# Dilated attention by token parity: four key blocks for every batch, probabilities divided before they are turned, values as the stationary operand

## The chip, the cores and the metric

One NeuronCore of a Trainium2 chip. The metric is the device time of the whole program in microseconds (us). The kernel before takes 1828.92 us, the median of 3 runs (1828.26 to 1829.07).

## The reference

A two-layer decoder trunk, 256 tokens, width 1024, float32. Each layer: RMSNorm, one input projection, multi-head latent attention (MLA, 8 heads) beside dilated window attention (3 groups of 8 heads), gates, output projection, then a dense feed-forward block (layer 0) or 8 experts (layer 1), then a gated embedding. The dilated part is what matters here:

```python
DIL_CONFIGS = ((128, 1), (512, 4), (2048, 16))     # window, dilation
# per group: tokens of one phase (token index modulo the dilation) attend to each other
dist = qi + span - kj
valid = (dist >= 0) & (dist <= span) & (blk * span - span + kj >= 0)
s = jnp.where(valid, q @ k * 64 ** -0.5 - slope * dilation * dist, -jnp.inf)
m = jnp.max(s); e = jnp.exp(s - m); den = jnp.sum(e)
o = (e / den) @ v;   lse = m + jnp.log(den)
# the three groups' outputs of head h are weighted by softmax over their lse
```

A weighting by the softmax of the three lse is the same as one softmax over the keys of all three groups together: one row of scores, one maximum, one sum. With dilation 4 or 16 a query sees only keys whose index has its own parity; with dilation 1 it sees the last 128 tokens of both parities.

## The kernel before

All big matrix products are made in three parts, high × high, high × low and low × high, from float32 halves. Weights come as a stream; ScalarE rounds each unit of 1024 words to its high half (`split_to`, L702), VectorE takes the rest as the low half (L1206), and `unit` on TensorE (L1874) runs 12 matmuls of 512 columns over it (L1885, L1886, L1911), for two token tiles. Rings of four units lie between them. No scheduler is at work: each engine's list is written out by hand in `attn`, once per layer, and semaphores bind the lists.

The change lies in the stretch of dilated attention. There `DIL_BATCHES` has 16 batches per layer, one for a query tile of 128 tokens and one head: tile 0 sees 128 keys in each of the three groups, tile 1 sees 256. Two batches (tile 0 of one head, tile 1 of its neighbour) share a pass of scores, one head in each half of the array's rows (`dil_term`, `scores_pair`, L2068). Then, per batch: `prep` on VectorE adds distances and masks and takes the maximum (L1365, L1369); `exps` on ScalarE (L820) makes the exponentials and their sum; `turn_probs` on TensorE transposes 3 or 6 blocks (L2093); `pt_evac` on ScalarE copies them (L831, L833); `values` on TensorE multiplies with the turned probabilities as the stationary tile and 64 columns of values moving (L2111); `normalise` on VectorE divides by the sum (L1382, L1383). When four batches are done, `o_dil_turn` transposes their two heads' outputs (L2149), and `od_round` and `od_rest` split them (L844, L1403). `round_pair` and `rest_pair` split the next two heads' queries and keys (L849, L1391).

Between these pieces TensorE runs "fill" units, the gate projections and then the branch projections (`FILL_AT`, `fill_unit`, `branch_unit`): one unit between two batches. `OM_AT`, `OD_AT` and `SPLIT_AT` say behind which batch the output turns and the splits stand. Before the stretch, V is projected by 12 units (`cols`, L1941) with contiguous blocks of 128 tokens as stationary tiles, and ScalarE scales it by the row's RMS factor while it copies it out (L777); the factors come from POOL (L515).

Of the kernel before, what the change touches and what calls it, by code (L numbers as in the profile page):

```python
# [22 lines left out]
P = 128  # L23
D = 1024
# [41 lines left out]
BRANCH_BANKS = ((2, 3), (0, 1), (7, 4), (2, 3))  # L66
# [31 lines left out]
def trunk_kernel(nc, x, p, positions, attn_norm, q_norm, kv_norm, ffn_norm, router_w, router_b, ple_norm,  # L98
                 final_norm, stream, out):
    ctx = ExitStack()  # L100
    with ctx:
# [33 lines left out]
        o_dil = sb("o_dil", [P, T, 512])  # L135
# [3 lines left out]
        dist = sb("dist", [P, DG, 256])  # L139
# [8 lines left out]
        rq8 = sb("rq", [P, 2, T])  # L148
        r2 = sb("r2", [P, T])
# [24 lines left out]
        merged = at("merged", [P, T, D], F32, Dr + 24576)  # L174
# [158 lines left out]

        layers = [Layer(f"l{i}", i) for i in range(2)]
# [154 lines left out]
        def _(g):  # L489
# [49 lines left out]
            link(g.iota(dint[:], [[-1, 256]], base=P, channel_multiplier=1))  # L539
# [5 lines left out]
            link(g.memset(cos[:], 0.0))  # L545
            g.sem_inc(const_ok, 1)
# [2150 lines left out]
```

## Time and profile before

| what | value |
|---|---|
| timed runs, median of 3 | 1828.92 us |
| profiled execution, span from first to last instruction | 1826.6 us |
| TensorE matmuls busy | 1817.6 us, 100% of the span |
| weight loads busy | 1524.3 us, 83% |
| VectorE, ScalarE, POOL busy | 81%, 68%, 8% |
| mean granted TensorE clock | 0.999 |

The page gives the profiled execution by its span alone; the timed runs are measured around the whole program, so they stand 2.3 us above it. Busy time of TensorE counts overlapping matmuls once, and each one's end is modelled, so 100% says that it had always something in flight. How fast it went is seen from the distance between starts. The dilated stretch lies at 168 to 249 us (layer 0) and at 711 to 792 us (layer 1).

### The profile page before, as it was taken

How to read it: one execution, taken by the hardware profiler on the slowest of the kernel's cores; microseconds unless marked ns; L12 is line 12 of the kernel's file. 1: busy time of each engine (PE TensorE's matmuls, PEld its weight loads, DVE VectorE, ACT ScalarE, POOL GpSimd, SP SyncE). 2: the span in 40 equal slices, each digit the busy share in tenths (PEclk: the TensorE clock that was granted, in tenths of full speed). 3: DMA queues.
4: the chain of work that ended last, by engine and by line, in shares of the span. 5: the costliest groups of instructions: out<-in, count | busy, mean ns of one | idle time of the engine just before them, and what ended most of it. 6: DMA issues, size and time to landing. Idle time of an engine off the chain costs nothing.

```text
span 1826.6 us, 27458 instructions
## 1 busy us (share of the span) xinstructions
PE 1817.6 (100%) x8998; PEld 1524.3 (83%) x8998; DVE 1470.6 (81%) x1695; ACT 1246.7 (68%) x1575; POOL 141.1 (8%) x202
## 2 busy tenths in 40 slices
PE   9999999999999999999999999999999999999998
PEld 8888888888888888888888888888888888888887
DVE  6566776665676556779999999999999999999998
ACT  6555565444456555657778788888887877878886
POOL 2400000000002200002200101001001010010000
PEclk9999999999999999999999999999999999999999
DMA  8643344555546543348999999999999999999993
GB/s 333 215 161 116 108 151 178 201 186 184 187 179 233 207 153 110 108 145 316 381 367 388 390 366 386 382 369 386 359 399 385 360 397 367 384 385 365 402 382 127
DMA packets 74066, 511.35 MB, mean 280 GB/s; under 512 B 8280, under 2 KB 8800, under 8 KB 14352
## 3 DMA queue, kind: packets, MB, share of 16 engines
q1 hardware_dynamic: 69072, 493.25, 70.3%
q0 software_dynamic: 4768, 16.95, 3.2%
q8 instruction: 41, 0.67, 0.2%
q10 hardware_dynamic: 160, 0.27, 0.0%
q14 instruction: 25, 0.20, 0.0%
HBM read 501.53 MB, written 8.91 MB: 279 GB/s over the span
## 4 chain that ended last, share of the span: by engine, by line
PE 99%; DVE 1%; DMA 0%; issue 0%; ACT 0%; DVEq 0%; POOL 0%; POOLq 0%; ACTq 0%
PE ps L1885 29%; PE ps L1911 29%; PE ps L1886 29%; PE ps L2111 2%; PE ps L2372 1%; PE ps L2093 1%; PE ps L2068 1%; PE ps L2044 1%; PE ps L1924 1%; PE ps L1926 1%; PE ps L1930 1%; PE ps L2054 1%; PE ps L2104 1%; PE ps L1949 1%; PE ps L2511 0%; PE ps L2270 0%
## 5 line engine op out<-in xcount | busy, mean ns | idle before, releaser
L1206 DVE TENSOR_TENSOR lo<-raw,hi 128x1024 fp32r<-128x1024 f32 (+1 forms) x940 | 1100.6, 1211 | 180.7 <-ACT hi L702 177.3
L702 ACT ACTIVATE hi<-raw 128x1024 fp32r<-128x1024 f32 (+1 forms) x940 | 969.4, 1051 | 312.5 <-PE ps L1911 304.0
L1885 PE MATMUL ps<-hi,hs_hi 128*128 128x512 f32 x896 | 355.4, 397 | 0.0
L1886 PE MATMUL ps<-hi,hs_lo 128*128 128x512 f32 x896 | 349.3, 390 | 0.0
L1885 PE MATMUL ps<-hi,hT_hi 128*128 128x512 f32 (+1 forms) x752 | 297.1, 396 | 0.0
L1886 PE MATMUL ps<-hi,hT_lo 128*128 128x512 f32 (+1 forms) x752 | 291.0, 388 | 0.0
L1911 PE MATMUL ps<-lo,hs_hi 128*128 128x512 f32 x896 | 276.4, 390 | 0.0
L1911 PE MATMUL ps<-lo,hT_hi 128*128 128x512 f32 (+1 forms) x752 | 199.5, 388 | 0.0
L1911 PEld LDWEIGHTS ps<-lo,hs_hi 128*128 128x128 f32 x896 | 168.1, 188 | 36.2 <-DVE lo L1206 0.2
L1885 PEld LDWEIGHTS ps<-hi,hs_hi 128*128 128x128 f32 x896 | 168.4, 188 | 33.2
L1886 PEld LDWEIGHTS ps<-hi,hs_lo 128*128 128x128 f32 x896 | 168.5, 188 | 33.1
L1885 PE MATMUL ps<-hi,eaT_hi 128*128 128x512 f32 x444 | 173.4, 391 | 0.0
L1886 PE MATMUL ps<-hi,eaT_lo 128*128 128x512 f32 x444 | 172.8, 389 | 0.0
L1911 PEld LDWEIGHTS ps<-lo,hT_hi 128*128 128x128 f32 x752 | 140.2, 188 | 29.4
L1885 PEld LDWEIGHTS ps<-hi,hT_hi 128*128 128x128 f32 x752 | 141.4, 188 | 27.1
L1886 PEld LDWEIGHTS ps<-hi,hT_lo 128*128 128x128 f32 x752 | 141.5, 188 | 26.8
L1911 PE MATMUL ps<-lo,eaT_hi 128*128 128x512 f32 x448 | 137.9, 389 | 0.0
L1911 PEld LDWEIGHTS ps<-lo,eaT_hi 128*128 128x128 f32 x448 | 84.0, 188 | 17.6
L1885 PEld LDWEIGHTS ps<-hi,eaT_hi 128*128 128x128 f32 x444 | 83.4, 188 | 17.0
L1886 PEld LDWEIGHTS ps<-hi,eaT_lo 128*128 128x128 f32 x444 | 83.3, 188 | 17.0
L1071 ACT ACTIVATE eaT_hi<-ps 128x512 fp32r<-128x512 f32 x54 | 32.4, 599 | 37.0 <-PE ps L2372 37.0
L820 ACT ACTIVATE pr<-pr,nmax 128x384 f32<-128x384 f32 (+2 forms) x64 | 39.1, 612 | 26.0 <-DVE nmax L1359 14.2
(358 smaller groups left out, 1765.5 us busy)
## 6 DMA issues: line engine op xcount, KB each, us to landing
raw<-in_stream SPq DMA_DIRECT2D x466, 1024.0 KB, 5.7
ybuf<-xs POOLq DMA_DIRECT2D x2, 1024.0 KB, 5.6
raw<-in_stream SPq DMA_DIRECT2D x3, 672.0 KB, 9.2
gain<-in_ffn_norm POOLq DMA_DIRECT2D x2, 512.0 KB, 7.9
gain<-in_ple_norm POOLq DMA_DIRECT2D x2, 512.0 KB, 6.8
hbuf<-hnf POOLq DMA_DIRECT2D x1, 1024.0 KB, 9.2
xs<-ybuf POOLq DMA_DIRECT2D x1, 1024.0 KB, 12.1
out_x<-hnat SPq DMA_DIRECT2D x3, 256.0 KB, 2.1
```

The lines of the kernel that those rows point to most:

```text
L702: a.activation(dst, src, ACT.Copy).then_inc(hi_done, 1)
L820: ins = a.activation(v, v, ACT.Exp, bias=nmax[:, n % 2, h:h + 1], accum_out=sums[:, n % 4, h:h + 1])
L1071: a.activation(eaT_hi[:], ps[:, 6, :].rearrange("p (k s) -> p k s", s=P), ACT.Copy).then_inc(e_hi, 1)
L1206: v.tensor_tensor(dst, src, h, ALU.subtract).then_inc(lo_done, 1)
L1885: pe.matmul(o, ah, wh[:, kk, :], start=(first and kk == 0), stop=False)
L1886: pe.matmul(o, al, wh[:, kk, :], start=False, stop=False)
L1911: ins = pe.matmul(ps[:, bank, c0:c0 + w], tile(l_hi, k0 + kk, t), wl[:, kk, :], start=False, stop=(last and kk == nk - 1))
L1924: pe.matmul(ps[:, outs[h] + t, 0:w], ah, wh[:, h, :], start=first, stop=False)
L1926: pe.matmul(ps[:, outs[h] + t, 0:w], al, wh[:, h, :], start=False, stop=False)
L1930: ins = pe.matmul(ps[:, outs[h] + t, 0:w], l_hi[:, k, P * t:P * t + P], wl[:, h, :], start=False, stop=last)
L1949: ins = pe.transpose(ps[:, 4 + j, P * k:P * k + P], src[:, t, CH * h + P * k:CH * h + P * k + P], ident[:])
L2111: ins = pe.matmul(ps[:, 6, 0:64], pT[:, n % 2, (t + 1) * m + k, :], vd[:, k, hd:hd + 64], start=(m == 0 and k == 0), stop=(m == DG - 1 and ...
```

## The change

The 256 tokens are taken in parity order: 128 even ones, then 128 odd ones. VectorE's copies of the turned queries and keys put them into that order. V is projected with stationary tiles that take every second token (`parity_block`), and its row factors are brought into the same order by two small matmuls against a shuffled identity (`norm_by_parity`, `unzip`, `rv`). A batch is now 128 queries of one parity and one head: 2 key blocks for dilation 1, one each for 4 and 16, so 4 blocks of 128 for every batch, one bank of scores. Both batches of a step are the two heads of a pair with the same parity.

The sum is now divided out of the probabilities by VectorE (`scale`), before they are turned. The product with the values changes its operands' roles: 64 columns of values are the stationary tile, the turned probabilities move with 128 columns, and the two heads write to partitions 0 to 63 and 64 to 127, in the array's two column halves (`values_pair`). The outputs are then already turned; `o_dil_turn` goes, and `normalise` remains for MLA only. Tables and batch loops give way to eight steps, written the same way on the three engines. On TensorE a step is: unit, scores, the 8 turns of the step before, unit, the values of the step before. A register that counts the experts' passes is also bounded below by one.

```diff
-BRANCH_BANKS = ((2, 3), (0, 1), (7, 4), (2, 3))
+BRANCH_BANKS = ((2, 3), (6, 5), (1, 4), (2, 3))
...
+NS = DH
+NB = NB_M + 2 * NS
+KEY_BLOCKS = [[(0, 0), (0, 1), (1, a), (2, a)] for a in range(2)]
+def batch(s, j):
+    return NB_M + 2 * s + j
+def prob_slot(n):
+    return n % 2 if n < NB_M else 2 * (((n - NB_M) // 2 + 1) % 2) + (n - NB_M) % 2
+def turn_bank(n):
+    return 7 if n < NB_M else 0 if n == NB - 1 else 4 + (n - NB_M) % 2
...
-pr = at("pr", [P, 2, 768], F32, Tr + 8192)
-pT = at("pT", [P, 2, 6, P], F32, Tr + 14336)
+pr = at("pr", [P, 4, CH], F32, Tr + 8192)
+pT = at("pT", [P, 2, 4, P], F32, Tr + 16384)
...
+def by_parity(row):
+    return row.rearrange("p (i a) -> p a i", a=2)
+def od_bank(hp):
+    return ps[:, 6 + hp % 2, 0:S].rearrange("p (a i) -> p a i", a=2)
 def score_bank(n):
...
+    return 2 + n % 2 if n < NB_M else (n - NB_M) % 2
...
+    link(g.tensor_copy(unzip[:], ident[:].rearrange("p (j a) -> p a j", a=2).unsqueeze(2).to_broadcast([P, 2, T, 64])))
...
+        a.wait_ge(rv_tr, i + 1)
+        for t in range(T):
+            rows = slice(64 * t, 64 * t + 64)
+            a.activation(rv[rows, i, :], ps[rows, 6, 0:4].rearrange("p (a t) -> p t a", t=T)[:, t, :],
+                         ACT.Copy).then_inc(rv_ok, 1)
+        a.wait_ge(rv_ok, T * i + T)
...
-                             scale=col(y.n1, t)).then_inc(y.ev_act, 1)
+                             scale=rv[:, i, t:t + 1]).then_inc(y.ev_act, 1)
...
         def pt_evac(n):
             a.wait_ge(y.ptr, n + 1)
...
+            if n >= NB_M:
+                a.wait_ge(y.pv, NB_M + (n - NB_M) // 2)
+            elif n >= 2:
                 a.wait_ge(y.pv, n - 1)
...
+            a.activation(pT[:, n % 2, :, :], ps[:, turn_bank(n), :].rearrange("p (b q) -> p b q", q=P),
                          ACT.Copy).then_inc(y.ptev, 1)
...
+        def od_round(hp):
+            a.wait_ge(y.pv, NB_M + 2 * hp + 2)
+            a.activation(by_parity(odT_hi[:, hp, :]), od_bank(hp), ACT.Copy).then_inc(y.ohi, 1)
...
+        for s in range(NS):
+            if s >= 3 and s % 2 == 1:
+                od_round(s // 2 - 1)
+            if s % 2 == 0:
+                gate_evac(s // 2, ACT.Copy, y.ev_act)
+            split_to(b + U_G + 2 * s + 8, **kw)
+            if s:
+                pt_evac(batch(s - 1, 0))
+                pt_evac(batch(s - 1, 1))
+            if s < T:
+                om_round(s)
+            exps(batch(s, 0))
+            exps(batch(s, 1))
+            split_to(b + U_G + 2 * s + 9, **kw)
+            if s % 2 == 0 and s < NS - 2:
+                round_pair(s // 2 + 1)
+        pt_evac(batch(NS - 1, 0))
+        pt_evac(batch(NS - 1, 1))
...
+                for t in range(T):
+                    ins = v.tensor_copy(d.rearrange("p k (a t j) -> p t k a j", a=2, t=T)[:, t],
+                                        ps[:, b0 + t, :].rearrange("p (k j a) -> p k a j", k=4, a=2))
+                ins.then_inc(y.tevac, 1)
...
+                s, j = (n - NB_M) // 2, (n - NB_M) % 2
+                a, h, slot = s % 2, 2 * (s // 2) + j, prob_slot(n)
+                for m, (d0, c0, c1) in enumerate(((1 - a, 0, 256), (3, 256, 384), (4, 384, CH))):
+                    ins = v.scalar_tensor_tensor(out=pr[:, slot, c0:c1].rearrange("p (c k) -> p c k", k=P),
+                                                 in0=dist[:, d0:d0 + (c1 - c0) // P, :], scalar=-SLOPES[m * DH + h],
+                                                 in1=ps[:, b0, c0:c1].rearrange("p (c k) -> p c k", k=P),
+                                                 op0=ALU.mult, op1=ALU.add)
                 link(ins)
...
+                v.tensor_reduce(nmax[:, n % 2, 0:1], pr[:, slot, :], AX.X, ALU.max,
                                 negate=True).then_inc(y.smax, 1)
+        def scale(n):
+            v.wait_ge(y.prob, n + 1)
+            link(v.reciprocal(rsum[:, n % 4, 0:1], sums[:, n % 4, 0:1]))
+            p_n = pr[:, prob_slot(n), :]
+            v.tensor_scalar(p_n, p_n, rsum[:, n % 4, 0:1], None, ALU.mult).then_inc(p_norm, 1)
...
-            v.tensor_tensor(odT_lo[:, k, :], ps[:, 5, 0:S], odT_hi[:, k, :], ALU.subtract).then_inc(y.olo, 1)
+            v.tensor_tensor(by_parity(odT_lo[:, k, :]), od_bank(k), by_parity(odT_hi[:, k, :]),
+                            ALU.subtract).then_inc(y.olo, 1)
...
+        for s in range(NS):
+            if s >= 3 and s % 2 == 1:
+                od_rest(s // 2 - 1)
+            prep(batch(s, 0))
+            prep(batch(s, 1))
+            split_to(b + U_G + 2 * s + 8, dyn)
+            if s < T:
+                om_rest(s)
+            scale(batch(s, 0))
+            scale(batch(s, 1))
+            if s % 2 == 0 and s < NS - 2:
+                rest_pair(s // 2 + 1)
+            split_to(b + U_G + 2 * s + 9, dyn)
...
+    def parity_block(src, k, t):
+        return by_parity(src[:, k, :])[:, t, :]
...
+        def norm_by_parity():
+            pe.wait_ge(const_ok, 2)
+            pe.wait_ge(y.n1.rs, y.n1.k + 1)
+            for a in range(2):
+                ins = pe.matmul(ps[:, 6, 2 * a:2 * a + T], unzip[:, a].rearrange("p r j -> p (r j)"),
+                                rx[:, y.n1.k, :], start=True, stop=True)
+            ins.then_inc(rv_tr, 1)
...
-            cols(b + U_V + 4 * j, dyn, hT_hi, hT_lo, (2 * (j % 2), 2 * (j % 2) + 1))
+            cols(b + U_V + 4 * j, dyn, hT_hi, hT_lo, (2 * (j % 2), 2 * (j % 2) + 1), tile=parity_block,
+                 after=(1, norm_by_parity) if j == 0 else None)
             if j == 0:
+                pe.wait_ge(rv_ok, T * i + T)
                 for t in range(T):
...
+        def dil_term(s, j, m, term):
+            hp, a = s // 2, s % 2
+            rows, q0 = slice(64 * j, 64 * j + 64), P * a
+            k0, k1 = (0, S) if m == 0 else (q0, q0 + P)
+            q_hi, k_hi = qk_hi[hp % 2][rows, 0, m, q0:q0 + P], qk_hi[hp % 2][rows, 1, m, k0:k1]
+            q_lo, k_lo = qT_lo[rows, 4 * m + hp, q0:q0 + P], kT_lo[rows, 4 * m + hp, k0:k1]
             q, k = ((q_hi, k_hi), (q_hi, k_lo), (q_lo, k_hi))[term]
...
+            c = (0, 256, 384)[m]
+            o = ps[:, score_bank(batch(s, j)), c:c + k1 - k0]
             return pe.matmul(o, q, k, start=(term == 0), stop=(term == 2))
...
+        def scores_pair(s):
+            pe.wait_ge(y.smax, batch(s, 0))
+            pe.wait_ge(y.qk_lo, 2 * (s // 2) + 2)
             for m in range(DG):
                 for term in range(3):
...
+                    first, second = dil_term(s, 0, m, term), dil_term(s, 1, m, term)
             first.then_inc(y.score, 1)
             second.then_inc(y.score, 1)
         def turn_probs(n):
...
+            if n < NB_M:
+                pe.wait_ge(y.prob, n + 1)
+                if n >= 1:
+                    pe.wait_ge(y.ptev, n)
+            else:
+                pe.wait_ge(p_norm, 2 * NS * i + (n - NB_M + 1))
...
+            for k in range(4):
+                ins = pe.transpose(ps[:, turn_bank(n), P * k:P * k + P], pr[:, prob_slot(n), P * k:P * k + P], ident[:])
             ins.then_inc(y.ptr, 1)
...
+        def values_pair(s):
+            hp, a = s // 2, s % 2
+            pe.wait_ge(y.ptev, batch(s, 1) + 1)
+            if hp == 0:
+                pe.wait_ge(y.oev, NB_M)
             else:
...
+                pe.wait_ge(y.olo, T + max(hp - 1, 0))
+            for n, (m, k) in enumerate(KEY_BLOCKS[a]):
+                for j in range(2):
+                    hd = 64 * (m * DH + 2 * hp + j)
+                    ins = pe.matmul(ps[64 * j:64 * j + 64, 6 + hp % 2, P * a:P * a + P], vd[:, k, hd:hd + 64], pT[:, j, n, :],
+                                    start=(n == 0), stop=(n == 3))
             ins.then_inc(y.pv, 1)
...
+                    evacuated(18)
+                    pe.wait_ge(y.olo, T)
+                branch_unit(x - 16, [(y.olo, T + 3), (y.ptev, batch(NS - 2, 1) + 1)] if x == 18 else None)
...
+        for s in range(NS):
+            fill_unit(3 + 2 * s)
+            scores_pair(s)
+            if s:
+                turn_probs(batch(s - 1, 0))
+                turn_probs(batch(s - 1, 1))
+            if s < T:
+                o_mla_turn(s)
+            fill_unit(4 + 2 * s)
+            if s:
+                values_pair(s - 1)
+        turn_probs(batch(NS - 1, 0))
+        turn_probs(batch(NS - 1, 1))
+        pe.wait_ge(y.olo, T + 2)
+        branch_unit(3, [(y.smax, NB), (y.ptev, batch(NS - 1, 0) + 1)])
+        values_pair(NS - 1)
         branch_unit(4)
         pe.wait_ge(y.olo, T + 4)
...
-        pe.reg_load(passes, npass[0:1, 0:1])
+        pe.reg_load(counted, npass[0:1, 0:1])
+        pe.reg_alu(passes, counted, 1, ALU.max)```

On TensorE, in the third and fourth batch of a layer, before: the end of the scores, turns (`pr` are the probabilities) and values, then a unit.

```order
L2068 MATMUL ps<-qk_hi_106,qT_lo 128x128
L2068 MATMUL ps<-qk_hi_106,qT_lo 128x256
L2093 MATMUL ps<-ident,pr 128x128 x6
L2111 MATMUL ps<-vd,pT 128x64 x3
L1885 MATMUL ps<-hi,hT_hi 128x512
```

And the next gap between two units, before:

```order
L1911 MATMUL ps<-lo,hT_hi 128x512 x4
L2141 MATMUL ps<-ident,o_mla 128x128 x4
L2093 MATMUL ps<-ident,pr 128x128 x3
L2111 MATMUL ps<-vd,pT 128x64 x6
L1885 MATMUL ps<-hi,hT_hi 128x512
```

The same engine with the change, in the fourth step, from the scores to the values. The order lists a float32 matmul once.

```order
L2120 MATMUL ps<-qk_hi_108,qT_lo 128x256 x2
L2120 MATMUL ps<-qk_hi_108 128x128 x2
L2120 MATMUL ps<-kT_lo,qk_hi_108 128x128 x2
L2120 MATMUL ps<-qk_hi_108,qT_lo 128x128 x2
L2120 MATMUL ps<-qk_hi_108 128x128 x2
L2120 MATMUL ps<-kT_lo,qk_hi_108 128x128 x2
L2120 MATMUL ps<-qk_hi_108,qT_lo 128x128 x2
L2144 MATMUL ps<-ident,pr 128x128 x8
L1918 MATMUL ps<-hi,hT_hi 128x512
```

```order
L1944 MATMUL ps<-lo,hT_hi 128x512 x4
L2169 MATMUL ps<-pT,vd 64x128 x8
L1918 MATMUL ps<-hi,hT_hi 128x512
```

All turns of a step now stand behind its scores, and the values alone fill the second gap, 8 matmuls where 3 and 6 stood in the two gaps.

On VectorE, before, from one pair of batches:

```order
L1365 SCALAR_TENSOR_TENSOR pr<-dist,ps 128x128 x3
L1369 TENSOR_REDUCE nmax<-pr 128x1
L1382 RECIPROCAL rsum<-sums 128x1
L1383 TENSOR_TENSOR o_dil<-ps,rsum 128x64
L1365 SCALAR_TENSOR_TENSOR pr<-dist,ps 128x256 x3
L1369 TENSOR_REDUCE nmax<-pr 128x1
L1206 TENSOR_TENSOR lo<-raw,hi 128x1024
L1382 RECIPROCAL rsum<-sums 128x1
L1383 TENSOR_TENSOR o_dil<-ps,rsum 128x64
```

And with the change, a step of two batches:

```order
L1394 SCALAR_TENSOR_TENSOR pr<-dist,ps 128x256
L1394 SCALAR_TENSOR_TENSOR pr<-dist,ps 128x128 x2
L1399 TENSOR_REDUCE nmax<-pr 128x1
L1230 TENSOR_TENSOR lo<-raw,hi 128x1024
L1405 RECIPROCAL rsum<-sums 128x1
L1407 TENSOR_SCALAR pr<-pr,rsum 128x512
L1405 RECIPROCAL rsum<-sums 128x1
L1407 TENSOR_SCALAR pr<-pr,rsum 128x512
L1424 TENSOR_TENSOR qT_lo<-qT,qk_hi_107 128x3x256
L1424 TENSOR_TENSOR kT_lo<-kT,qk_hi_107 128x3x256
L1230 TENSOR_TENSOR lo<-raw,hi 128x1024
```

The small division of each output (64 columns, behind the values) has become a division of the probabilities (512 columns, ahead of the turns). The first three rows stand twice in a row in a step.

## Rows read from the trace of the kernel before

**Rows 1.** The page, section 1 (busy us, share, instructions) and the chain by engine.
```profile
PE 1817.6 (100%) x8998; PEld 1524.3 (83%) x8998; DVE 1470.6 (81%) x1695; ACT 1246.7 (68%) x1575; POOL 141.1 (8%) x202
...
PE 99%; DVE 1%; DMA 0%; issue 0%; ACT 0%; DVEq 0%; POOL 0%; POOLq 0%; ACTq 0%
```

**Rows 2.** Busy time by stretch: PE, PEld, DVE, ACT, POOL; clock, DMA share, GB/s.
```profile
167.84:249.15 81.31, 81.31 (x570) 69.68 (x570) 57.78 (x124) 52.36 (x94) 0.00 (x0) 1.00 0.32 115
710.60:791.90 81.30, 81.30 (x570) 69.70 (x570) 57.44 (x124) 52.37 (x94) 0.00 (x0) 1.00 0.33 115
```

**Rows 3.** The chain of waits in layer 0's projections: start us, us, what.
```profile
73.84 0.91 PE ps L1911 x4
...
76.56 0.91 PE ps L1911 x4
```

**Rows 4.** Timeline of PE, first score group: start us, us, line, operands, shapes.
```profile
166.85 1.07 PE L1911 MATMUL ps<-lo,hT_hi 128*128 128x512 f32 x4
167.84 0.39 PE L2068 MATMUL ps<-qk_hi 64*128 64x128 f32 x2
168.01 0.34 PE L2068 MATMUL ps<-kT_lo,qk_hi 64*128 64x128 f32 x2
...
168.79 0.39 PE L2068 MATMUL ps<-qk_hi,qT_lo 64*128 64x128 f32 x2
169.11 0.50 PE L1885 MATMUL ps<-hi,hT_hi 128*128 128x512 f32 x1
169.44 0.40 PE L1886 MATMUL ps<-hi,hT_lo 128*128 128x512 f32 x1
```

**Rows 5.** Timeline of PE, turns, values and the unit behind them.
```profile
181.01 0.49 PE L2093 MATMUL ps<-ident,pr 128*128 128x128 f32 x3
181.34 1.45 PE L2111 MATMUL ps<-vd,pT 128*128 128x64 f32 x12
182.60 0.48 PE L1885 MATMUL ps<-hi,hT_hi 128*128 128x512 f32 x1
182.91 0.39 PE L1886 MATMUL ps<-hi,hT_lo 128*128 128x512 f32 x1
...
184.53 1.08 PE L1911 MATMUL ps<-lo,hT_hi 128*128 128x512 f32 x4
```

**Rows 6.** Timeline of PE, MLA scores with 256 columns.
```profile
126.69 1.03 PE L2054 MATMUL ps<-kmT,qmT 96*128 96x256 f32 x4
127.55 0.60 PE L2093 MATMUL ps<-ident,pr 128*128 128x128 f32 x4
```

**Rows 7.** Timeline of PE, second matmul behind the last dilated output turn.
```profile
249.38 0.39 PE L1886 MATMUL ps<-hi,omT_lo 128*128 128x512 f32 x1
```

**Rows 8.** Timeline of POOL, the row factors of layer 0.
```profile
21.69 1.63 POOL L515 TENSOR_TENSOR rx<-ms,nhalf 128x2 f32<-128x2 f32 x1 [2.81 <-DVE ms L1241]
```

**Rows 9.** Timeline of PE, start of the fourth V unit.
```profile
31.80 0.39 PE L1885 MATMUL ps<-hi,hT_hi 128*128 128x512 f32 x1
```

**Rows 10.** Timeline of ACT behind its square pass.
```profile
27.65 2.94 ACT L702 ACTIVATE hi<-raw 128x1024 fp32r<-128x1024 f32 x3
```

**Rows 11.** Groups on DVE by shape, whole run: count, busy us, mean ns, idle before.
```profile
L1206 DVE TENSOR_TENSOR lo<-raw,hi 128x1024 fp32r<-128x1024 f32 x916 | 1081.3, 1221 | 162.1 <-ACT hi L702 159.0
L1365 DVE SCALAR_TENSOR_TENSOR pr<-dist,ps 128x256 f32<-128x256 f32 x48 | 17.2, 413 | 0.0
L1365 DVE SCALAR_TENSOR_TENSOR pr<-dist,ps 128x128 f32<-128x128 f32 x48 | 10.9, 282 | 23.4 <-PE ps L2068 23.4
L1391 DVE TENSOR_TENSOR kT_lo<-kT,qk_hi 128x768 fp32r<-128x768 f32 x8 | 7.6, 952 | 0.0
L1359 DVE TENSOR_REDUCE nmax<-pr 128x2 f32<-128x512 f32 x8 | 5.5, 687 | 0.3
L1382 DVE RECIPROCAL rsum<-sums 128x1 f32<-128x1 f32 x32 | 5.2, 163 | 16.8 <-PE ps L2111 16.8
L1640 DVE TENSOR_SCALAR hnf<-hnat,rx 128x1024 f32<-128x1024 f32 x2 | 1.4, 750 | 0.1
```

More of the change, by code:

```diff
@@ L134, in trunk_kernel @@
         o_mla = sb("o_mla", [P, T, 512])
-        o_dil = sb("o_dil", [P, T, 512])
+        pp1 = sb("pp1", [P, T, 512])
+        unzip = at("unzip", [P, 2, T, 64], F32, om_at + 4096)
         ident = sb("ident", [P, P])
@@ L414, in lat_pairs @@
             return ([(lat[:, t, 0:QR], pr[:, t, 0:QR]) for t in range(T)]
-                    + [(lat[:, t, QR:LAT], pr[:, t, QR:LAT]) for t in range(T)])
+                    + [(lat[:, t, QR:LAT], pr[:, T + t, 0:KVR]) for t in range(T)])
         def unit_views(u, src, dst):
@@ L556, in dist_masks @@
                 g.wait_ge(trig_ok, 1)
-                for m in range(DG):
+                for m in range(3, 2 + DG):
                     link(g.affine_select(out=dist[:, m, :], in_=dist[:, m, :], compare_op=ALU.is_ge, fill=BIG,
-                                         base=P, pattern=[[-1, 256]], channel_multiplier=1))
-                link(g.affine_select(out=dist[:, 0, :], in_=dist[:, 0, :], compare_op=ALU.is_ge, fill=BIG,
-                                     base=0, pattern=[[1, 256]], channel_multiplier=-1))
+                                         base=0, pattern=[[-2, P]], channel_multiplier=2))
+                near = dist[:, 0:3, :]
+                link(g.affine_select(out=near, in_=near, compare_op=ALU.is_ge, fill=BIG,
+                                     base=1, pattern=[[-1, 3], [-2, P]], channel_multiplier=2))
+                link(g.affine_select(out=near, in_=near, compare_op=ALU.is_ge, fill=BIG,
+                                     base=P - 1, pattern=[[1, 3], [2, P]], channel_multiplier=-2))
             def rotate(dst, t, n):
@@ L1932, in wide_unit, with cols @@
                 ins.then_inc(used, 1)
-            def cols(u, dyn, l_hi, l_lo, outs, w=CH, nku=2, units=4, ready=None, turn_between=None, turn_beside=None):
+            def parity_block(src, k, t):
+                return by_parity(src[:, k, :])[:, t, :]
+            def cols(u, dyn, l_hi, l_lo, outs, w=CH, nku=2, units=4, ready=None, turn_between=None, turn_beside=None,
+                     tile=token_block, after=None):
                 for h in range(units):
@@ L1940, in cols @@
                     beside = (lambda: x_turn(*turn_beside[1:])) if turn_beside and h == turn_beside[0] else None
-                    unit(u + h, dyn, l_hi, l_lo, (nku, w), nku * h, outs, 0, h == 0, h == units - 1, free=free, beside=beside)
+                    unit(u + h, dyn, l_hi, l_lo, (nku, w), nku * h, outs, 0, h == 0, h == units - 1, tile=tile, free=free,
+                         beside=beside)
+                    if after and h == after[0]:
+                        after[1]()
             def turn_tiles(src, trs, ready, base, which=(0, 1, 2, 3)):
```

216 lines of the change are left out of this document (46 added, 170 removed).

## The prediction

> **What bounds the kernel now.** I read the page first. TensorE's matmuls cover the whole span and 99% of the chain that ended last is its own work; no other engine is busy for more than 81% [rows 1]. Then the engines' busy time over the stretch that the change rewrites, once in each layer: 81.3 us each time, TensorE busy in all of it, VectorE in 58 of them, ScalarE in 52, the DMA queues a third busy, clock 1.00 [rows 2]. In the timeline of that stretch each TensorE row starts before the row above it has ended [rows 4, 5]. So time is won or lost only where TensorE's own list gets shorter or longer, or where another engine becomes so late that TensorE stands still, which happens nowhere in this stretch now. I therefore price the list by the distance from one start to the next, not by an instruction's length.
>
> **Prices.** Two plain units of 12 matmuls end 2.72 us apart, 0.227 for a 512-column matmul [rows 3]. Behind other work the first eight come every 0.231 (182.91 to 184.53, 7 steps), so such a unit costs 2.76 [rows 5]. One float32 matmul is two records in the trace: the order lists 3 and 6 for values where the trace has 6 and 12.
> - Scores of two heads: from the last four matmuls before them (166.85) to the second one behind (169.44) are 2.59; less 5 × 0.227 leaves 1.46 for the group. Its 9 pairs come every 0.119 (167.84 to 168.79 is 8 steps), 1.07 in all, so 0.39 is the price of going over to half arrays and back [rows 4].
> - Transposes: three in 0.33 (181.01 to 181.34), 0.11 each [rows 5].
> - Values: 12 records from 181.34 to 182.60, 0.105 each, 0.21 for a matmul [rows 5].
> - A 256-column float32 record takes 0.215 (126.69 to 127.55, four): its columns set it, so 128 columns are 0.107 of streaming [rows 6]. At 64 columns it is still 0.105, so there the load of the 128-column stationary tile sets it.
>
> **The stretch as a sum, per layer.** From 166.85 to 249.38 are 82.53 us [rows 4, 7]; less 5 × 0.227 and 16 units × 2.76 leaves 37.3 for all that isn't a unit. Of it 8 score groups are 8 × 1.46 = 11.7, and 72 + 8 + 8 transposes (probabilities, MLA outputs, dilated outputs) × 0.111 are 9.8. The remaining 15.8 are the values: 72 × 0.21 = 15.1, and 0.7 for the slow first matmul behind their groups.
>
> **What the change takes and adds, per layer.**
> - Scores: still 9 pairs a group, now 3 with 256 columns in both halves and 6 with 128 in both (before, 128 beside 256 in each). The 128-column half steps at 0.111 (168.01 to 168.79, 7 steps), the pair at 0.119 [rows 4], so 6 × 0.008 = 0.05 a group: −0.4. Bounds: 0; and, if pairs of 128 columns were bound by their columns alone (0.06 each), −2.8. I stay near the row, since a half alone already has 128 columns there.
> - Probability transposes: 64 for 72, −0.9. The dilated outputs come out turned, so 8 transposes go, −0.9.
> - Values: 8 groups of 8 matmuls (16 records, 64-column stationary tile, 128 columns moving), two heads in the two column halves. The trace before has no column halves. The nearest rows are the two heads in row halves, one pair every 0.111 to 0.119 [rows 4]. The two records of one matmul follow each other in the trace, so the halves overlap with an offset of one record: 8.5 steps × 0.115 = 0.98, and 0.39 for the change of tiling, about 1.38 a group, 11.0 for 8 against 15.8: −4.8. Bounds: 1.1 (8 steps of 0.107 and two thirds of the switch), and with no overlap 16 × 0.11 + 0.39 = 2.15. I take the pair row because it is the same kind of pairing on the same engine.
> - V projection: two small float32 matmuls bring the row scales into parity order, 4 records of 0.105 and a slow follower: +0.45. They wait for nothing: POOL writes the scales at 21.7 to 23.3, their place is behind the second V unit, at 31.80 − 2.72 = 29.1 [rows 3, 8, 9]. ScalarE ends its square pass at 27.65 and must now wait for them and make two small copies, to about 30.0; the first split behind it ends at 31.05, and the fourth V unit, which needs it, starts at 31.80 + 0.45 [rows 9, 10]. Hidden with 1.2 us to spare; what is later than that is paid one for one.
> - V's stationary tiles are read with a step of two words. A load takes 0.105 and lies under 0.227 of matmul; it may double at no cost. I take 0.
> - One more register operation behind the experts: +0.1 in the whole program.
>
> That is −7.0 per layer, −14.0 in two, then +0.9 and +0.1.
>
> **Waits.** VectorE now divides the probabilities (a reciprocal and a 512-column multiply) before TensorE may turn them. Behind the end of a score group it has two preps of 0.41 + 2 × 0.28 + 0.69 = 1.66, a split of 1.22, and two divisions of 0.16 + 0.45 (the multiply halfway between 0.16 for one column and 0.75 for 1024): 5.8 us [rows 11]. TensorE comes to that turn after 0.9 + 2.76 + 1.38 + 2.76 + 1.41 = 9.2, so 3.4 of slack. A whole step is 3.3 + 2.4 + 1.2 = 7.0 on VectorE, 8.9 where the next pair of heads is split (2 × 0.95) [rows 11], against 9.2 on TensorE. Behind a late turn a unit would be queued, whose weights are split long before. Only at the end of the stretch there is one unit less between scores and turn: TensorE is there after 0.9 + 2.76 + 1.38 = 5.0, the second division is ready at 5.8, its turn would begin at 5.5. +0.3 a layer, +0.6.
>
> Sum: −14.0 + 0.9 + 0.1 + 0.6 = −12.4. The profiled span is 1826.6; the timed median of 1828.9 lies 2.3 above it, which I take as lying around the span and unchanged. So 1814.2 for the span and 1816.5 for the time.
>
> **A rule against it, and one on its size.** The rows show loads of a full array lying under its matmuls: at 64 columns the step is 0.105, not 0.105 + 0.053 [rows 5]. The Trainium skill ("TensorE: Matmul & The Clock Gate", section The mechanism) says that a weight load overlaps matmuls in flight only when its row group differs; column halves share all rows. By that rule the second rival below would come, at 1841.6. For full tiles the row contradicts it; for halves no run here shows either. The same page (Measured speedup vs the span model) gives 2.38 for three column tiles. An estimate from that page, 2 × 2.38 / 3 = 1.6 for two halves, would make a group 16 × 0.11 / 1.6 + 0.39 = 1.5 and the time 1818.4.
>
> **Rivals.**
> 1. The halves don't overlap, one streams while the other waits: 2.15 a group, 0.77 × 16 = 12.3 more, nearly the whole gain, 1828.8. For it: each half streams float32 from all 128 rows, twice what a row half reads. Against: two streams at once are what the score pairs show. A partial overlap, 1.6 to 1.9, gives 1820 to 1825.
> 2. Slower: the halves' loads are not hidden. Each record pays its load (half of 0.105) and its 0.107: 16 × 0.16 + 0.39 = 2.95 a group, 1.57 × 16 = 25.1 more, 1841.6. It decides from 2.15 a group on, where the gain is used up. Against it is the hidden load of full tiles.
> 3. VectorE's division makes TensorE wait at each turn. VectorE goes from 71% of the stretch to about 87%. It would take 3.4 us more than I count; if steps stretched from 9.2 to 10.0, 14 × 0.8 = 11 are lost, 1828. Against: its other work is done most of a step ahead of need.
> 4. The change doesn't do what it says, because V's spread loads cost four times the contiguous ones: 0.42 for 0.227 over 288 matmuls, +56. No row shows a spread load.
>
> **Chances.** Forecast (group 1.1 to 1.6) 0.70, its own range 1811 to 1820; partial overlap or some waits 0.10 (1820 to 1825); no gain 0.09 (1825 to 1832, within 0.2%, about what a measurement of this kernel tells from no change); slower 0.11 (unhidden loads 0.08, the rest 0.03). So faster 0.80, same 0.09, slower 0.11. The range for eight in ten reaches from 1811 (groups at 1.2 and half of the bound on the scores) to 1829.
>
> **What would show it.** In the profile after: 16 value records within about 1.0 us, groups of 1.3 to 1.5 between units; the stretch 7 us shorter, about 74.5; no wait of TensorE before turns but the last; V matmuls still every 0.227; VectorE's step below 9.2. Value records at 0.11 from start to start would be rival 1, at 0.16 or more rival 2, a standstill before each turn rival 3. A V projection slower than 2.72 a unit would break my zero for the spread loads.

## The result: the stretch got shorter, the rest of the program longer

| | median of the timed runs | profiled span |
|---|---|---|
| before | 1828.59 us (1827.78 to 1829.07, 4 runs) | 1826.6 us |
| with the change | 1837.75 us (1837.69 to 1838.47, 4 runs) | 1835.9 us |

All timings compared below ran at a granted clock of 0.999 or 1.000, but for one of the ten of e4_before_all128 (0.752, 2268.40 us), which is left out.

The ratio is 1.0052, 95% interval 1.004 to 1.0064: the change costs 9.2 us where I had forecast a gain of 12.4. The page after, first the busy time of the engines, then the chain that ended last by engine, answers to [rows 1]:

```profile
PE 1827.4 (100%) x8942; PEld 1506.3 (82%) x8942; DVE 1475.3 (80%) x1707; ACT 1245.2 (68%) x1563; POOL 142.0 (8%) x203
...
PE 99%; DVE 1%; issue 0%; ACT 0%; POOL 0%; DVEq 0%; POOLq 0%; ACTq 0%
```

TensorE has 56 matmuls fewer and is busy for 9.8 us more. No other engine has taken the end of the program over. So some matmuls must have become dearer. The first place to look is the rewritten stretch. TensorE's timeline after (start us, us, line, operands, shapes), the first score group and a little later the turns and the first values, answers to [rows 4, 5]:

```profile
168.09 1.07 PE L1944 MATMUL ps<-lo,hT_hi 128*128 128x512 f32 x4
169.09 0.39 PE L2120 MATMUL ps<-qk_hi 64*128 64x256 f32 x2
...
170.05 0.28 PE L2120 MATMUL ps<-qk_hi,qT_lo 64*128 64x128 f32 x2
170.26 0.66 PE L2202 MATMUL ps<-ident,o_mla 128*128 128x128 f32 x4
...
170.98 0.39 PE L1919 MATMUL ps<-hi,hT_lo 128*128 128x512 f32 x1
...
177.50 1.09 PE L2144 MATMUL ps<-ident,pr 128*128 128x128 f32 x8
178.43 0.60 PE L2202 MATMUL ps<-ident,o_mla 128*128 128x128 f32 x4
...
180.72 1.07 PE L1944 MATMUL ps<-lo,hT_hi 128*128 128x512 f32 x4
181.72 1.09 PE L2169 MATMUL ps<-pT,vd 128*64 128x128 f32 x16
...
183.08 0.40 PE L1919 MATMUL ps<-hi,hT_lo 128*128 128x512 f32 x1
```

The 16 value records take 1.02 us from the first to what follows them. The group costs 2.36 (180.72 to 183.08) less 5 × 0.227, so 1.23. The score group costs 2.89 (168.09 to 170.98) less 5 × 0.227 and four turns of 0.111, so 1.31. The end of the layer's stretch:

```profile
240.32 1.09 PE L2169 MATMUL ps<-pT,vd 128*64 128x128 f32 x16
...
241.69 0.40 PE L1919 MATMUL ps<-hi,omT_lo 128*128 128x512 f32 x1
```

From 168.09 to 241.69 are 73.6 us, where [rows 4, 7] had 82.53: 8.9 us less in each layer (layer 1: 705.96 to 779.55). So the stretches won nearly 18 us, and the program still lost 9: some 27 us were spent elsewhere. Most of them were spent here. TensorE's timeline in an expert, before and then after:

```profile
1000.18 0.39 PE L1885 MATMUL ps<-hi,hs_hi 128*128 128x512 f32 x1
...
1001.09 0.62 PE L1911 MATMUL ps<-lo,hs_hi 128*128 128x512 f32 x2
1001.54 0.39 PE L1885 MATMUL ps<-hi,hs_hi 128*128 128x512 f32 x1
```

```profile
1009.15 0.39 PE L1918 MATMUL ps<-hi,hs_hi 128*128 128x512 f32 x1
...
1010.08 0.64 PE L1944 MATMUL ps<-lo,hs_hi 128*128 128x512 f32 x2
1010.55 0.39 PE L1918 MATMUL ps<-hi,hs_hi 128*128 128x512 f32 x1
```

Six matmuls of the same pattern take 1.36 us before and 1.40 after. Nothing waits between them, and the code for them has not changed. By the mean distance between starts, over the whole run, the 512-column matmuls of the experts went from 227.9 to 235.0 ns (`hi` with `hs_hi`), 227.7 to 230.4 (`hs_lo`), 227.5 to 233.5 (`lo` with `hs_hi`), 896 of each (the first ones behind other work left out of the means); from 226.8 to 236.1, 226.8 to 230.4 and 226.7 to 232.0 for `eaT_hi`, `eaT_lo` and `lo` with `eaT_hi`, 448 of each; and the dense block's, 112 of each, from 226.8 to some 233. That makes 14.1 + 8.2 + 2.0 = 24.3 us, and the two things that V's projection adds, 0.9 and 1.9 (below), bring it to 27.1. The units over `hT` outside of V stayed at 227 to 229.

What sets these apart is where their stationary tiles lie. In the program's memory plan the rings `hi` and `lo` and the tiles `hT` begin at an address, within a partition, that is 128 modulo 256 bytes, before and after. `hs`, `eaT`, `faT` and most tiles of the branches lie in regions behind the small tables. `dist` grew smaller by 512 bytes and the new `rv` and the rounding gave 128 back, so these regions moved down by 384 bytes: from 128 modulo 256, as the rings, to 0. Below, the distance is the address of the stationary tile less that of the moving words, modulo 256 bytes; it was 0 and became 128.

### The profile page after: what moved, and what is told of

The parts are those of the page before. It is cut to its first block, busy times and chain, and to the rows that moved or that the text cites. A ratio compares the mean times of both kernels' runs of the same rounds, so it can differ in the third digit from the quotient of the medians.

```text
span 1835.9 us, 27322 instructions
## 1 busy us (share of the span) xinstructions
PE 1827.4 (100%) x8942; PEld 1506.3 (82%) x8942; DVE 1475.3 (80%) x1707; ACT 1245.2 (68%) x1563; POOL 142.0 (8%) x203
## 4 chain that ended last, share of the span: by engine, by line
PE 99%; DVE 1%; issue 0%; ACT 0%; POOL 0%; DVEq 0%; POOLq 0%; ACTq 0%
PE ps L1918 29%; PE ps L1944 29%; PE ps L1919 29%; PE ps L2407 1%; PE ps L2144 1%; PE ps L2120 1%; PE ps L2096 1%; PE ps L2169 1%; PE ps L1957 1%; PE ps L1959 1%; PE ps L1963 1%; PE ps L2106 1%; PE ps L2154 1%; PE ps L1990 1%; PE ps L2547 0%; PE ps L2430 0%
## 5 line engine op out<-in xcount | busy, mean ns | idle before, releaser
L1230 DVE TENSOR_TENSOR lo<-raw,hi 128x1024 fp32r<-128x1024 f32 (+1 forms) x940 | 1103.1, 1211 | 189.1 <-ACT hi L724 185.4
L1918 PE MATMUL ps<-hi,hs_hi 128*128 128x512 f32 x896 | 360.4, 402 | 0.0
L1919 PE MATMUL ps<-hi,hs_lo 128*128 128x512 f32 x896 | 352.3, 393 | 0.0
L1918 PE MATMUL ps<-hi,hT_hi 128*128 128x512 f32 (+1 forms) x752 | 298.0, 397 | 0.0
L1919 PE MATMUL ps<-hi,hT_lo 128*128 128x512 f32 (+1 forms) x752 | 291.7, 389 | 0.0
L1944 PE MATMUL ps<-lo,hs_hi 128*128 128x512 f32 x896 | 282.0, 395 | 0.0
L1944 PEld LDWEIGHTS ps<-lo,hs_hi 128*128 128x128 f32 x896 | 168.6, 188 | 40.2
L1944 PE MATMUL ps<-lo,hT_hi 128*128 128x512 f32 (+1 forms) x752 | 200.1, 388 | 0.0
L1918 PEld LDWEIGHTS ps<-hi,hs_hi 128*128 128x128 f32 x896 | 168.6, 188 | 38.2
L1919 PEld LDWEIGHTS ps<-hi,hs_lo 128*128 128x128 f32 x896 | 168.9, 189 | 35.4
L1918 PE MATMUL ps<-hi,eaT_hi 128*128 128x512 f32 x444 | 177.1, 399 | 0.0
L1919 PE MATMUL ps<-hi,eaT_lo 128*128 128x512 f32 x444 | 174.5, 393 | 0.0
L1918 PEld LDWEIGHTS ps<-hi,hT_hi 128*128 128x128 f32 x752 | 142.0, 189 | 28.8 <-issue 1.7
L1944 PEld LDWEIGHTS ps<-lo,hT_hi 128*128 128x128 f32 x752 | 140.8, 189 | 29.1
L1919 PEld LDWEIGHTS ps<-hi,hT_lo 128*128 128x128 f32 x752 | 142.2, 189 | 26.9
L1944 PE MATMUL ps<-lo,eaT_hi 128*128 128x512 f32 x448 | 140.4, 394 | 0.0
L1944 PEld LDWEIGHTS ps<-lo,eaT_hi 128*128 128x128 f32 x448 | 84.1, 188 | 19.9
L1918 PEld LDWEIGHTS ps<-hi,eaT_hi 128*128 128x128 f32 x444 | 83.6, 188 | 20.5
L1919 PEld LDWEIGHTS ps<-hi,eaT_lo 128*128 128x128 f32 x444 | 83.7, 188 | 18.8
L1749 DVE TENSOR_TENSOR e_act<-e_sig,ps 128x512 f32<-128x512 f32 x56 | 38.5, 688 | 26.8 <-PE ps L1944 26.3
```

What stands on the lines that cost most here:

```text
L1230: v.tensor_tensor(dst, src, h, ALU.subtract).then_inc(lo_done, 1)
L1749: v.tensor_tensor(e_act[:], e_sig[:], ps[:, 1, :], ALU.mult).then_inc(e_actd, 1)
L1918: pe.matmul(o, ah, wh[:, kk, :], start=(first and kk == 0), stop=False)
L1919: pe.matmul(o, al, wh[:, kk, :], start=False, stop=False)
L1944: ins = pe.matmul(ps[:, bank, c0:c0 + w], tile(l_hi, k0 + kk, t), wl[:, kk, :], start=False, stop=(last and kk == nk - 1))
```

## The experiments

Theory A: the place of the stationary tile, modulo some power of two, sets the pace. Theory B: it is the new code or its register. Four kernels ran together.

**e1_old_places**, the changed kernel with the regions moved back by 384 bytes:

```diff
+        top[0] += 384
         qk_odd = region(6144)
```

> The changed kernel with 384 bytes left free ahead of the working regions, so that all stationary tiles behind them (hs, eaT, faT, latT, peT) lie at the addresses of the kernel before. Theory A, place: the change is worth what I forecast in its stretch (-12) and lost 21 us because these tiles moved by 384 bytes (from 128 to 256, modulo 512, while the moving ring stayed at 128), so their matmuls come every 0.231 to 0.233 instead of 0.227. It expects 1816 to 1818 and 0.227 in the experts. Rival B, code: TensorE's list (a register more, other positions of instructions) slows the loops; it expects 1837 to 1838 as before this edit.

1812.97 us (1812.66 to 1813.4, 5 runs), ratio to before 0.9916, interval 0.9903 to 0.993. One line of padding gives back 24.8 us, and the change is a gain of 15.4. The experts' matmuls step at 226.7 to 228.1 ns again. The stretch takes 73.4 us:

```profile
167.99 1.07 PE L1945 MATMUL ps<-lo,hT_hi 128*128 128x512 f32 x4
...
241.38 0.40 PE L1920 MATMUL ps<-hi,omT_lo 128*128 128x512 f32 x1
```

**e2_plus128**, the same with `top[0] += 128`:

> The changed kernel with 128 bytes left free there: the tiles lie at 384 modulo 512, the ring at 128. If what counts repeats every 256 bytes, 1816 to 1818; if every 512 bytes, or if only the exact old addresses are good, 1836 to 1839. Rival B: 1837 to 1838.

1813.11 us (ratio 0.9916, 0.9901 to 0.9931). The tiles now lie 256 bytes from those of e1_old_places and cost the same: the price repeats after 256 bytes, and not after 128.

**e3_before_shift128**, the kernel before, with its regions moved by 128 bytes and the register bound of the change, which makes it a test of B too:

```diff
+        top[0] += 128
         qk_odd = region(6144)
...
-                pe.reg_load(passes, npass[0:1, 0:1])
+                pe.reg_load(counted, npass[0:1, 0:1])
+                pe.reg_alu(passes, counted, 1, ALU.max)
```

> The kernel before with 128 bytes left free ahead of the regions (tiles at 256 modulo 512, ring at 128), and with the register bound of the change. Theory A: 1828.6 + 20 = 1847 to 1851, experts at 0.231 to 0.233. Rival B: 1828 to 1829, or the +9 of the register alone, 1838.

1852.74 us, ratio 1.0135 (1.0119 to 1.015). The kernel before has all its own code but for the register bound and is 24.3 us slower; its timeline in an expert shows the step of the changed kernel, 1.40 for six:

```profile
1005.09 0.40 PE L1886 MATMUL ps<-hi,hs_hi 128*128 128x512 f32 x1
...
1006.02 0.63 PE L1912 MATMUL ps<-lo,hs_hi 128*128 128x512 f32 x2
1006.49 0.40 PE L1886 MATMUL ps<-hi,hs_hi 128*128 128x512 f32 x1
```

**e4_before_all128**, the same, but with the 128 bytes ahead of `hi`, so that rings and tiles move together:

> The kernel before with 128 bytes left free ahead of the moving ring, so that ring, hT and all tiles behind lie at 256 modulo 512 together; register bound as in the change. If the distance between stationary and moving operand counts: 1828 to 1829. If the address itself counts: all matmuls slow, hT's too, 1828.6 + 20 + 11 = about 1860. Rival B: 1828 to 1829.

1828.10 us, ratio 0.9998 (0.9988 to 1.0008). The rings and all these tiles are at 0 modulo 256 now and it costs nothing, nor does the register bound. Six matmuls take 1.36 us:

```profile
999.77 0.39 PE L1886 MATMUL ps<-hi,hs_hi 128*128 128x512 f32 x1
...
1001.13 0.39 PE L1886 MATMUL ps<-hi,hs_hi 128*128 128x512 f32 x1
```

Not the place counts but the distance from the stationary tile to the moving words. Theory B has fallen.

Then four variants of e1_old_places, run together (before: 1827.82 us, 9 runs).

**e5_plus64** and **e6_plus32** change the rounding of the regions (shown for 64; the other has 32 in both places):

```diff
-            top[0] = (top[0] + 127) // 128 * 128
+            top[0] = (top[0] - 64 + 127) // 128 * 128 + 64
```

> The changed kernel with the stationary tiles 64 bytes away from the place where they ran at 1812.97 us (distance to the moving units 64 modulo 256). Theory A1, only the distance of 128 is slow: 1813 and hs_hi stepping at 228 ns. Theory A2, the price grows with the distance: about half of the 24.7 us, 1825, hs_hi at 231 to 232 ns. Theory A3, only equal places are fast: 1837.

> The same with 32 bytes. A1: 1813. A2: a quarter of 24.7 us, 1819. A3: 1837.

1820.72 us (ratio 0.9961, 0.9947 to 0.9975) and 1840.51 (1.0069, 1.0052 to 1.0086). The expectations name the wrong distances: the rounding went down, so the tiles stand 64 and 96 bytes below the old place, at distances of 192 and 160 modulo 256. Above the 1812.97 of distance 0 the price is 7.8 us at 192, 27.5 at 160 and 24.8 at 128. A1 and A3 are wrong and A2 is at best half right: the price does not simply grow with the distance.

**e7_v_contiguous** takes the two-word step out of V's stationary reads:

```diff
-                    cols(b + U_V + 4 * j, dyn, hT_hi, hT_lo, (2 * (j % 2), 2 * (j % 2) + 1), tile=parity_block,
+                    cols(b + U_V + 4 * j, dyn, hT_hi, hT_lo, (2 * (j % 2), 2 * (j % 2) + 1),
```

> At the old places, V projected with contiguous blocks of 128 tokens as stationary tiles (its rows then stand in token order and not in parity order, so the values are those of other keys; the amount of work is the same). If the two-word step of the stationary reads makes the V matmuls step at 233 instead of 227 ns, 288 x 6.5 ns = 1.9 us go: 1811.1 against 1812.97. If the step costs nothing, as I predicted: no change.

1811.33 us (ratio 0.991, 0.9893 to 0.9926), 1.6 below e1_old_places, from another chip; the spans differ by 1.3, and measured each against its own runs of the kernel before the difference is 1.1. So the time alone gives 1.1 to 1.6. The rows are clearer: layer 0's V matmuls step at 227.5 ns in the mean and in e1_old_places at 233.6, which is 1.8 us over all 288. In the first V unit four matmuls take 0.91 us, in the changed kernel's 0.93:

```profile
26.05 1.08 PE L1945 MATMUL ps<-lo,hT_hi 128*128 128x512 f32 x4
26.96 0.39 PE L1919 MATMUL ps<-hi,hT_hi 128*128 128x512 f32 x1
```

```profile
23.20 0.39 PE L1918 MATMUL ps<-hi,hT_hi 128*128 128x512 f32 x1
...
25.07 1.09 PE L1944 MATMUL ps<-lo,hT_hi 128*128 128x512 f32 x4
26.00 0.39 PE L1918 MATMUL ps<-hi,hT_hi 128*128 128x512 f32 x1
...
27.87 1.09 PE L1944 MATMUL ps<-lo,hT_hi 128*128 128x512 f32 x4
28.80 0.50 PE L2050 MATMUL ps<-rx,unzip 128*128 128x2 f32 x4
...
29.50 0.40 PE L1919 MATMUL ps<-hi,hT_lo 128*128 128x512 f32 x1
```

**e8_values_by_head** sends each head's four value matmuls in a row:

```diff
-                    for n, (m, k) in enumerate(KEY_BLOCKS[a]):
-                        for j in range(2):
+                    for j in range(2):
+                        for n, (m, k) in enumerate(KEY_BLOCKS[a]):
```

> At the old places, each head's four value matmuls one after another instead of alternating between the two column halves. If the halves overlap only because neighbours in the list stand in different halves: a group grows from 1.02 us of records to 16 x 0.107 = 1.7, so 16 groups cost 11 us more, 1824. If records of one half can follow each other as fast as alternating ones, or the overlap reaches across: 1813.

1820.26 us (ratio 0.9957, 0.9943 to 0.9971), 7.3 more than e1_old_places. Its values, and below them those of e1_old_places:

```profile
181.36 1.58 PE L2170 MATMUL ps<-pT,vd 128*64 128x128 f32 x16
182.87 0.50 PE L1919 MATMUL ps<-hi,hT_hi 128*128 128x512 f32 x1
```

```profile
181.56 1.09 PE L2170 MATMUL ps<-pT,vd 128*64 128x128 f32 x16
182.59 0.50 PE L1919 MATMUL ps<-hi,hT_hi 128*128 128x512 f32 x1
```

1.51 us for 16 records against 1.03; 16 groups × 0.48 = 7.7. The starts of the single records, alike in all 16 groups to some nanoseconds, say how. In the alternating order two records, one of each half, start 0.007 apart, and the next two 0.109 behind them. Head by head, each half takes a record every 0.109 as well, but the second head's first record starts 0.006 behind the fifth of the first head. So a half needs 0.109 a record in either order, as I had priced it (0.107), and the two halves work at once in both: here for half of each head's records, in the alternating order for all. Both outcomes that I had named were wrong; the overlap reaches across, but only over the last four records.

**e9_place_alone** measures the disputed price by itself, in one execution. Groups of four units (48 matmuls) per place, the moving words in one ring, eight tiles:

```python
for tl in tiles:                          # at 0, 32, ... 224 bytes from the moving words
    units(plain(tl), 4)
units(spread(tiles[0]), 4)                # every second word of the tile at distance 0
```

> Not the kernel, only its units (this leaves the whole computation out): groups of 48 matmuls with 512 float32r columns, their stationary tiles at distances of 0, 32, 64, 96, 128, 160, 192 and 224 bytes modulo 256 from the moving words, first with TensorE alone, then with VectorE and ScalarE reading and writing 1024-word slots as in the splits. Theory P (TensorE's own two reads collide): the pitch depends on the distance already when TensorE is alone, 227 at 0 and 231 to 236 ns at 32 and 128. Theory Q (its reads collide with the other engines' accesses): 227 ns at every distance alone, and differences only in the second half. The last group of each half reads the tiles with a step of two words: 233 ns if that step costs what it does in the V projection.

Busy time by stretch (PE, PEld, DVE, ACT, POOL; clock, DMA share, GB/s); each stretch is one group, so its length is the time of 48 matmuls. In order: 0, 32, 64, 128, 192, the spread tile, and then 0 and 32 again with VectorE and ScalarE at work (96, 160 and 224 took 11.24, 11.20 and 11.20):

```profile
38.92:49.81 10.89, 10.89 (x49) 9.01 (x48) 0.00 (x0) 0.00 (x0) 0.00 (x0) 1.00 0.01 2
49.81:61.00 11.19, 11.19 (x49) 9.02 (x48) 0.00 (x0) 0.00 (x0) 0.00 (x0) 1.00 0.00 0
61.00:72.20 11.20, 11.20 (x49) 9.02 (x48) 0.00 (x0) 0.00 (x0) 0.00 (x0) 1.00 0.01 1
...
83.44:94.60 11.16, 11.16 (x49) 9.04 (x48) 0.00 (x0) 0.00 (x0) 0.00 (x0) 1.00 0.00 0
...
105.80:116.79 10.99, 10.99 (x49) 9.02 (x48) 0.00 (x0) 0.00 (x0) 0.00 (x0) 1.00 0.00 0
...
127.99:139.19 11.20, 11.20 (x49) 9.26 (x48) 0.00 (x0) 0.00 (x0) 0.00 (x0) 1.00 0.01 1
139.19:150.08 10.89, 10.89 (x49) 9.01 (x48) 10.68 (x10) 10.62 (x11) 0.00 (x0) 1.00 0.00 0
150.08:161.27 11.19, 11.19 (x49) 9.02 (x48) 11.19 (x11) 11.19 (x13) 0.00 (x0) 1.00 0.01 2
```

Per matmul: 226.9 ns at distance 0; 233.1, 233.3, 234.2, 232.5, 233.3 from 32 to 160; 229.0 at 192; 233.3 at 224; 233.3 for the spread tile. It is the same to 0.01 us a group of plain tiles with both other engines busy for 95% of the time and more, and the clock is 1.00 throughout. Q falls: TensorE alone shows the whole price. That its two reads collide, as theory P has it, fits, but no row shows a collision. The DMA queues were nearly still here (share 0.01); with them at 0.9 and more, in the experts, the prices are about the same: e5_plus64 at distance 192 steps its expert matmuls at 229 ns, e6_plus32 at 160 at 233 to 234, the changed kernel at 128 at 230 to 236, 233 in the mean.

**e10_spread_and_shifted**, again one execution, asks for the period, for spread tiles at other distances, and whether the distance alone decides:

```python
for d in (0, 32, 64, 96, 128, 160, 192, 224):
    units(spread(tiles[d]), 4)
for d in (256, 320):
    units(plain(tiles[d]), 4)
for d in (96, 0, 224, 32):                # the moving words themselves shifted by 96 bytes
    units(plain(tiles[d]), 4, odd)
```

> Again only units of 12 matmuls with 512 columns and TensorE alone (the computation is left out). First the two-word-step tiles at distances of 0, 32, ... 224 bytes: if the step and the distance are two prices that add, 233 ns at distance 0 and more elsewhere; if there is one collision that can happen or not, 233 at all of them. Then plain tiles at 256 and 320 bytes: 226.8 and 233.4 if the period is 256 bytes, as at 0 and 64. Then the moving words themselves shifted by 96 bytes, with tiles at 96, 0, 224 and 32: if the distance decides, 226.8 (distance 0), 233.4 (160), 232.5 (128) and 229.1 (192); if the tile's own place decides, 234.2, 226.8, 233.3 and 233.1.

Busy time by stretch (PE, PEld, DVE, POOL; clock, DMA share, GB/s), for spread tiles at 0 and 64, plain ones at 256 and 320, and with the shifted moving words the tiles at 96, 0 and 32 (that at 224 took 11.20 too):

```profile
35.63:46.83 11.20, 11.20 (x49) 9.27 (x48) 0.00 (x0) 0.00 (x0) 1.00 0.00 1
57.96:69.00 11.04, 11.04 (x49) 9.32 (x48) 0.00 (x0) 0.00 (x0) 1.00 0.01 1
...
124.91:135.80 10.89, 10.89 (x49) 9.01 (x48) 0.00 (x0) 0.00 (x0) 1.00 0.01 2
135.80:147.00 11.20, 11.20 (x49) 9.02 (x48) 0.00 (x0) 0.00 (x0) 1.00 0.00 0
147.00:157.92 10.92, 10.92 (x49) 9.01 (x48) 0.00 (x0) 0.00 (x0) 1.00 0.01 2
157.92:169.12 11.20, 11.20 (x49) 9.01 (x48) 0.00 (x0) 0.00 (x0) 1.00 0.00 0
...
180.32:191.29 10.97, 10.97 (x49) 8.83 (x47) 0.00 (x0) 0.00 (x0) 1.00 0.01 1
```

256 costs what 0 does and 320 what 64 does: the period is 256 bytes. With the moving words shifted, the tile at 96 (distance 0) is a fast one, 10.92, and the tile at 0 (distance 160) a slow one, 11.20; the tile at 32 (distance 192) comes out at 10.97 and that at 224 (distance 128) at 11.20. The distance decides, not the tile's own place; the largest difference to e9_place_alone is 0.8 ns a matmul, at distance 128. A spread tile has other good distances than a plain one: 64 is its best, 230.0 ns, 0 gives 233.3, and the others 231.5 to 233.5. The two prices don't add.

## Why the prediction was wrong

- **The failed step** is one that was not there: the sum has terms for what the change computes, none for what it moves in memory. The diff shows `dist` shrinking and `rv` coming in ahead of the regions, and I took "Prices" from rows of before, 0.227 for a 512-column matmul, as if it belonged to the operation. It belongs to the operation at a distance of 0 modulo 256; at 128 the same matmuls took 3 to 9 ns more, 24.3 us for 4368 of them. Price of the omission by the timed runs: 24.8 us (1837.75 less 1812.97). All four rivals were in the rewritten stretch or in V; none of them is what came.
- **The values**: forecast 1.38 a group, measured 1.23, 1.2 us a layer more than I had counted. Rival 1 (2.15) and rival 2 (2.95) did not come. The two column halves went in step like the row halves, a pair every 0.109 where I took 0.115 and half a step more; the rest is the change of tiling, 0.35 for 0.39. The rule of the Trainium skill ("TensorE: Matmul & The Clock Gate", section The mechanism), that a load overlaps matmuls only of another row group, does not hold for these column halves: in each of them a record with its own load comes every 0.109, no more than the 0.107 that 128 columns take to stream [rows 6]. The estimate from the Trainium skill's table on that page (section Measured speedup vs the span model), 1.5 a group, was too high as well.
- **The scores**: forecast 1.41 a group, measured 1.31. From a group's first record to what follows it are 1.26 us in the kernel before and 1.17 after, 0.09 less, where I had counted 0.05. The rest is a price of before that I read too high: I took the one group whose follower is a 512-column matmul. The first such matmul behind half arrays takes 0.34 for 0.227, the first turn only 0.17 for 0.11, and seven of eight groups are followed by turns. What was too much on the scores of before was missing on its values.
- **Turns and output turns**: 8 turns in 0.93 (177.50 to 178.43), 16 fewer a layer, as counted.
- **The stretch by its records**, from each start to the next, per layer before and after: scores 10.1 and 9.4, turns 9.9 and 7.8, values 15.0 and 8.2, 512-column matmuls 47.6 and 48.3. So it won 8.9 where I had 6.7: 0.3 more on the scores, 0.6 on the turns and their wait, 1.3 on the values with the changes of tiling around them.
- **V's row factors**: 27.87 to 29.50 is 1.63, less 5 × 0.233 leaves 0.46, forecast 0.45. ScalarE's small copies ended at 29.7 and nobody on TensorE waited for them.
- **V's spread loads**: I took 0; my own mark "slower than 2.72 a unit" came. Its first unit took 2.80 (23.20 to 26.00), 233.3 ns for 226.9 [rows 3], 24 units: +1.9, of which e7_v_contiguous won 1.1 to 1.6 back. The Trainium skill ("SBUF — State Buffer", section Specifications (TRN2)) asks for two accesses to each 16-byte line, which a step of two float32 words still makes. By that rule the loads would be free; at a distance of 0 they were not, and at 64 half of the price was gone (e10_spread_and_shifted), so here the measurement decides.
- **VectorE and the waits**: VectorE was busy for 60.4 of 74.9 us, 81% for the 87% I had feared. The turns inside the stretch wait for no division. At the last turns the wait that I forecast is there, but smaller: the last division ends at 236.88, the first turn behind it starts at 236.94, 0.17 behind the turn before it, and the next one 0.17 behind that, for 0.11 each elsewhere. That is 0.1 a layer for the 0.3 I had counted; the idle column of the profile shows nothing of it. The division of 512 columns took 0.487, forecast 0.45. First its group, then the stretch, then VectorE's last division and the last turns:

```profile
L1407 DVE TENSOR_SCALAR pr<-pr,rsum 128x512 f32<-128x512 f32 x32 | 15.6, 487 | 1.1
...
168.10:243.00 74.90, 74.90 (x548) 59.83 (x547) 60.42 (x128) 53.06 (x89) 0.00 (x0) 1.00 0.35 127
...
236.40 0.48 DVE L1407 TENSOR_SCALAR pr<-pr,rsum 128x512 f32<-128x512 f32 x1
...
236.38 1.21 PE L2144 MATMUL ps<-ident,pr 128*128 128x128 f32 x8
```

At the old distances the terms add up: two stretches of −9.1 (82.53 to 73.39; −18.3), V's factors +0.9 and its spread loads +1.9 give −15.5, and 1812.97 is 15.4 below before. So without the omission the gain of 12.4 would have been 3.0 short: the stretches won 4.8 more than I had counted (9.1 for 6.7, twice) and the spread loads took 1.9 of it back, two errors that partly offset each other. The 2.3 us between span and time, last, compared a median with another execution; within one execution it is 1.7 to 1.8. The mechanism in the stretch was right, and better than priced; the forecast's sign was wrong because of a side effect outside it.

## What stays open

Why a distance of 0 is free, 192 nearly so and the others not, I can't say; no run shows what happens between the two reads. Nor is it shown why within one unit the matmuls are hit unequally (`hi` with `hs_hi` 235.0, `hi` with `hs_lo` 230.4, both tiles at the same distance). The fastest kernel here whose V rows are the right ones is e1_old_places. A plan in which V's reads also run at full pace needs its tokens written in parity order, and wasn't tried, nor was V with its tiles at distance 64. Only float32r operands were measured.

## What to carry to other kernels

When a change resizes any buffer, compare the address of every later one with the plan before, and pin the distance between stationary tiles and moving words (here 0 modulo 256 bytes) in the code rather than leave it to the allocator. When a change moves the time and the stretch it rewrote did what was forecast, compare the distance from start to start of the untouched, most frequent instruction: 3 to 9 ns on 4368 matmuls, too small to be seen in one row, was more than the change itself was worth. Small matmuls in two column halves should alternate between the halves in the list.

## What the runs showed of the hardware

- A 512-column float32r matmul with a 128 × 128 float32r stationary tile steps at 226.9 ns when tile and moving words are 0 modulo 256 bytes apart in their partitions, and at 229.0 to 234.2 ns at the other seven multiples of 32 below 256; VectorE and ScalarE at work beside it change nothing.
- A stationary tile read with a step of two words has its own good distances: 233.3 ns at 0, 230.0 at 64.
- Float32 matmuls of 64 × 128 stationary and 128 columns: a record every 0.109 us in each column half, its load hidden. Two halves work at once: 16 records take 1.02 us when they alternate in the list, and 1.51 when one half's eight stand before the other's.
- Going over between a full array and halves: a 512-column matmul ahead of half-array records takes 0.32 for 0.227, what follows the last of them starts 0.20 to 0.21 behind it, and a first 512-column matmul behind them takes 0.34, a first turn 0.17 for 0.11.
